# Cross products packed with the diagonal ones, the group norm's sum and its matmul one slab earlier, masks from ScalarE

## The reference, cut to what matters

```python
seg = a_cum[:, :, :, None] - a_cum[:, :, None, :]
decay = exp(where(tril, seg, -inf))          # within a chunk
scores = einsum("bcign,bcjgn->bcijg", C, B)
y_diag = einsum("bcijgr,bcjgrp->bcigrp", scores[..., None] * decay, x * dt)
# from one chunk to the next: states carried with exp of the sums, both directions
v = (y * silu(z)).reshape(b, l, 8, 256)      # group norm
v = v * rsqrt(mean(v * v, axis=-1) + EPS) * g
```

## Time and profile before

| | us |
|---|---|
| median of 3 runs | 2915.68 |
| lowest, highest | 2913.25, 2916.30 |
| the profiled execution | 2910.87 |
| its span, first to last instruction | 2909.1 |
| PE busy | 2869.3 (99%) |
| DVE busy | 1867.6 (64%) |
| ACT busy | 1310.2 (45%) |

### The profile page before, as it was taken

How to read it: one execution, slowest core, us unless ns; L and a number is a source line. 1 busy time by engine, 2 the same in 40 slices (tenths; PEclk the granted TensorE clock), 3 DMA queues, 4 the chain that set the end, 5 groups by cost and what they waited for, 6 DMA issues and landing times.

```text
span 2909.1 us, 34457 instructions
## 1 busy us (share of the span) xinstructions
PE 2869.3 (99%) x12914; PEld 2315.9 (80%) x12914; DVE 1867.6 (64%) x2387; ACT 1310.2 (45%) x1805; POOL 139.5 (5%) x237
## 2 busy tenths in 40 slices
PE   7999999999999999999999999999999999999998
PEld 5888877777778888888888888777777788888887
DVE  5444479999997654444554436889999866554445
ACT  5322256666664434222342224566676534442223
POOL 1000001110001000000000000100100010000000
PEclk9999999999999999999999999999999999999999
DMA  6333233333335433333333333333333463333332
GB/s 194 97 97 95 81 93 100 106 101 96 104 91 180 110 102 94 96 98 96 94 104 99 94 100 95 91 92 90 103 103 96 116 180 92 95 108 95 101 90 84
DMA packets 532024, 301.88 MB, mean 104 GB/s; under 512 B 17039, under 2 KB 521751, under 8 KB 531895
## 3 DMA queue, kind: packets, MB, share of 16 engines
q1 hardware_dynamic: 511888, 261.65, 31.8%
q0 software_dynamic: 17296, 37.29, 4.3%
q10 hardware_dynamic: 2711, 1.21, 0.2%
HBM read 280.54 MB, written 19.53 MB: 103 GB/s over the span
## 4 chain that ended last, share of the span: by engine, by line
PE 83%; ACT 0%; issue 0%; DMA 0%; POOL 0%; DVE 0%; ACTq 0%
PE bank L1270 78%; PE bank L1425 2%; PE bank L1461 1%; PE bank L1401 0%; PE bank L1416 0%; PE bank L1477 0%; PE bank L1469 0%; PE bank L1408 0%; PE bank L1502 0%; DMA LB<-l_image 0%; ACT hhi L800 0%; PE bank L1305 0%; PE bank L1321 0%; POOL RB L401 0%; ACT o_tm L866 0%
## 5 line engine op out<-in xcount | busy, mean ns | idle before, releaser
L1270 PE MATMUL bank<-uhi,whi 128*128 128x512 f32 x1952 | 767.9, 393 | 13.4 <-DVE ulo L938 11.2
L877 DVE TENSOR_TENSOR wlo<-wraw,whi 128x1024 fp32r<-128x1024 f32 x496 | 605.9, 1223 | 266.8 <-ACT whi L505 256.8
L1270 PE MATMUL bank<-hhi,whi 128*128 128x512 f32 x1952 | 767.9, 393 | 2.2 <-ACT tg L710 2.2
L1270 PE MATMUL bank<-ulo,whi 128*128 128x512 f32 x1952 | 761.0, 390 | 0.0
L1270 PE MATMUL bank<-hlo,whi 128*128 128x512 f32 x1952 | 760.7, 390 | 0.0
L1270 PE MATMUL bank<-hhi,wlo 128*128 128x512 f32 x1952 | 760.5, 390 | 0.0
L1270 PE MATMUL bank<-uhi,wlo 128*128 128x512 f32 x1952 | 760.5, 390 | 0.0
L505 ACT ACTIVATE whi<-wraw 128x1024 fp32r<-128x1024 f32 x496 | 521.5, 1054 | 422.6 <-PE bank L1270 405.7
L1270 PEld LDWEIGHTS bank<-uhi,whi 128*128 128x128 f32 x1952 | 367.0, 188 | 101.3 <-issue 11.7
L1270 PEld LDWEIGHTS bank<-hhi,whi 128*128 128x128 f32 x1952 | 366.8, 188 | 89.8 <-issue 11.7
L1270 PEld LDWEIGHTS bank<-uhi,wlo 128*128 128x128 f32 x1952 | 367.0, 188 | 77.4
(11 more groups left out here) (212 smaller groups left out, 1902.3 us busy)
## 6 DMA issues: line engine op xcount, KB each, us to landing
wraw<-in_ffn_w_up SPq DMA_DIRECT2D x179, 512.0 KB, 3.8
wraw<-in_w_in SPq DMA_DIRECT2D x160, 512.0 KB, 4.0
wraw<-in_ffn_w_down SPq DMA_DIRECT2D x64, 512.0 KB, 3.8
wraw<-in_ssd_w_out SPq DMA_DIRECT2D x32, 512.0 KB, 4.4
wraw<-in_ffn_w_down SPq DMA_DIRECT2D x32, 384.0 KB, 3.3
y_spill<-yz POOLq DMA_DIRECT2D x16, 512.0 KB, 3.3
yraw<-y_spill POOLq DMA_DIRECT2D x32, 256.0 KB, 3.9
wraw<-in_conf_w_out SPq DMA_DIRECT2D x16, 512.0 KB, 4.5
```

What stands on the lines that cost most here:

```text
L877: v_.tensor_tensor(wlo[:, t % RING, :], wraw[:, t % RING, :], f32(whi[:, t % RING, :]), ALU.subtract).then_inc(lo_ready, 1)
L1270: ins = t_.matmul(out, a[:, slot, w], b[:, at + k, :], start=start and k == 0 and a is whi and b is hi, stop=stop and k == nk - 1 and a is ...
```

## The change

1. The cross products of a request come right behind its four diagonal ones, in `seg_diag`, into bank4 and bank5 instead of bank2 and bank6. `seg_cross` is gone. ACT takes all six exponentials of a request in step 1 or 3. `seg_diag(0)` waits for both copies of the scores out of banks 4 and 5, and `y_rows(0)`, which writes bank4, for all exponentials of request 1.
2. ACT writes two masks more, into bank2 and bank3, in step 0 behind its copies of the transposed x, in all but the first SSD tile of a layer. PE adds masks in that first tile alone: 8 mask matmuls in all instead of 36.
3. The group norm's sum on DVE moves from the start of step 1 to step 0, behind the taps and ahead of `split`. Its matmul on PE moves from step 1, behind the slab, to step 0, behind the transposes, and goes to bank0 where there is an SSD; there it waits for ACT's read of the slab in bank0, and the slab of step 2 waits for ACT's Ln. In group 9 the matmul stays in step 1 and in bank4.
4. The transposes are written as one accumulation group for each bank.

```diff
@@ ACT, step 0, group with ssd
                             a_.activation(xT[:, 2 * b:2 * b + 2, :], ..., ACT.Copy).then_inc(xt_ready, 1)
+                        if H % NG:
+                            act.wait_ge(xt_ready, H * 2 + 2)
+                            for d in range(2):
+                                mask(0, d)
...
                     if ssd and t in (1, 3):
-                        for e in range(4):
+                        for e in range(EPR):
                             decay(t // 2, e)
-                    if ssd and t in (2, 4):
-                        for e in range(4, EPR):
-                            decay(t // 2 - 1, e)
@@ DVE
-                    if t == 1 and norm:
-
-                        dve.wait_ge(gsq, n * 2 + 2)
-                        v_.tensor_tensor(sq[:, 0, :], sq[:, 0, :], sq[:, 1, :], ALU.add).then_inc(gsq_sum, 1)
...
+                    if t == 0 and norm:
+                        dve.wait_ge(gsq, n * 2 + 2)
+                        v_.tensor_tensor(sq[:, 0, :], sq[:, 0, :], sq[:, 1, :], ALU.add).then_inc(gsq_sum, 1)
@@ PE, seg_diag
-                    by_act = 2 if r else 1 if H % NG else 0
+                    by_act = r or H % NG
...
+                        ins = t_.matmul(bank[4 + c][:, :], LB[rows, H % 2, 1, r, :], RB[rows, H % 2, r, :], start=True, stop=True)
+                        if by_act:
+                            ins.then_inc(seg_ps, 1)
+                    if not by_act:
+                        for c in range(2):
+                            for d in range(2):
+                                t_.matmul(heads(2 + 4 * c + d), identr[:, :], never[:, d, :]..., start=False, stop=True)...
@@ PE, group
                         pe.wait_ge(*free[t])
+                        if t == 2 and norm and ssd:
+                            pe.wait_ge(gln, n + 1)
...
-                    if t == 1 and norm:
+                    if t == (0 if ssd else 1) and norm:
                         pe.wait_ge(gsq_sum, n + 1)
                         if ssd:
-                            pe.wait_ge(sc_ready, H * 2 + 1)
-                        t_.matmul(bank[4][:, :], ones[:, :], sq[:, 0, :], start=True, stop=True).then_inc(gst_ps, 1)
+                            pe.wait_ge(*((tg_ready, G + 1) if slabs else (gate_ready, L * 2 * KD + gate + 1)))
+                        t_.matmul(bank[0 if ssd else 4][:, :], ones[:, :], sq[:, 0, :], start=True, stop=True).then_inc(gst_ps, 1)
                     if t == 1 and ssd:
                         pe.wait_ge(xt_ready, H * 2 + 2)
+                        pe.wait_ge(sc_ready, H * 2 + 2)
...
-                    if t == 2 and ssd:
-                        seg_cross(0)
...
                     if t == 4 and ssd:
-                        seg_cross(1)
-                        if norm:
-                            pe.wait_ge(gln, n + 1)
-                        pe.wait_ge(sc_ready, H * 2 + 2)
+                        pe.wait_ge(e_ready, H * EPG + EPG)
                         y_rows(0)
```

More of the change, by code:

```diff
@@ L258, in masks_by @@
             L, tile = divmod(H, NG)
-            return L * (6 * NG - 2) + 6 * tile + 4 * r
+            return L * (8 * NG - 4) + 8 * tile + 4 * r
         def seg_rows(c, d):
@@ L682, in decay @@
                     else:
-                        dst, src = M[:, r, e - 4, :, 5 - e, :], bank[2 + 4 * (e - 4)]
+                        dst, src = M[:, r, e - 4, :, 5 - e, :], bank[e]
                     a_.activation(dst, src[:, :].rearrange("p (h i) -> p h i", h=HPG), ACT.Exp).then_inc(e_ready, 1)
@@ L730, in group @@
                         need(act, y2_ready, n * 2)
-                        a_.activation(rbc[:, :], bank[4][:, :], ACT.Ln, scale=1.0 / GF, bias=eps_t[:, 0:1]).then_inc(gln, 1)
+                        a_.activation(rbc[:, :], bank[0 if ssd else 4][:, :], ACT.Ln, scale=1.0 / GF, bias=eps_t[:, 0:1]).then_inc(gln, 1)
                         act.wait_ge(gln, n + 1)
@@ L1399, in seg_diag @@
                         for d in range(2):
-                            rows, masked = seg_rows(c, d), c >= 2 - by_act
+                            rows = seg_rows(c, d)
                             ins = t_.matmul(bank[2 + 4 * c + d][:, :], LB[rows, H % 2, 0, r, :], RB[rows, H % 2, r, :],
-                                            start=not masked, stop=masked, skip_group_check=masked)
-                            if r:
+                                            start=not by_act, stop=bool(by_act), skip_group_check=bool(by_act))
+                            if by_act:
                                 ins.then_inc(seg_ps, 1)
[L1405 to L1411, removed]
                     for c in range(2):
-                        pe.wait_ge(e_ready, H * EPG + r * EPR + 2 * c + 1)
                         rows = seg_rows(1 - c, c)
-                        t_.matmul(bank[2 + 4 * c][:, :], LB[rows, H % 2, 1, r, :], RB[rows, H % 2, r, :], start=True, stop=True).then_inc(seg_ps, 1)
+                        ins = t_.matmul(bank[4 + c][:, :], LB[rows, H % 2, 1, r, :], RB[rows, H % 2, r, :], start=True, stop=True)
+                        if by_act:
+                            ins.then_inc(seg_ps, 1)
+                    if not by_act:
+                        for c in range(2):
+                            for d in range(2):
+                                t_.matmul(heads(2 + 4 * c + d), identr[:, :], never[:, d, :].unsqueeze(1).broadcast_to([P, HPG, P]),
+                                          start=False, stop=True).then_inc(seg_ps, 3 if c and d else 1)
                 def y_rows(r):
@@ L1468, in group @@
                             for j in range(2):
-                                ins = t_.transpose(bank[2 + c // 2][:, (c % 2) * GF + j * P:(c % 2) * GF + (j + 1) * P],
-                                                   bc[:, 2 + j, chunk(c)], ident[:, :])
+                                ins = t_.matmul(bank[2 + c // 2][:, (c % 2) * GF + j * P:(c % 2) * GF + (j + 1) * P],
+                                                bc[:, 2 + j, chunk(c)], ident[:, :], start=c % 2 == 0 and j == 0, stop=c % 2 == 1 and j == 1,
+                                                is_transpose=True, skip_group_check=True)
                             if c % 2:
                                 ins.then_inc(xt_ps, 1)
-                    if t == 1 and norm:
+                    if t == (0 if ssd else 1) and norm:
                         pe.wait_ge(gsq_sum, n + 1)
                         if ssd:
-                            pe.wait_ge(sc_ready, H * 2 + 1)
-                        t_.matmul(bank[4][:, :], ones[:, :], sq[:, 0, :], start=True, stop=True).then_inc(gst_ps, 1)
+                            pe.wait_ge(*((tg_ready, G + 1) if slabs else (gate_ready, L * 2 * KD + gate + 1)))
+                        t_.matmul(bank[0 if ssd else 4][:, :], ones[:, :], sq[:, 0, :], start=True, stop=True).then_inc(gst_ps, 1)
                     if t == 1 and ssd:
                         pe.wait_ge(xt_ready, H * 2 + 2)
+                        pe.wait_ge(sc_ready, H * 2 + 2)
                         pe.wait_ge(seg_in[H % 2], (H // 2 + 1) * 8 * 16)
                         seg_diag(0)
-                    if t == 2 and ssd:
-                        seg_cross(0)
                     if t == 3 and ssd:
```

## The result

| | before | changed |
|---|---|---|
| median of 4 runs, us | 2915.24 | 2963.68 |
| lowest to highest | 2913.25 to 2916.30 | 2961.15 to 2964.94 |
| span of the profiled execution | 2909.1 | 2963.0 |
| granted clock, mean | 0.996 | 0.987 |

The changed kernel is slower: ratio 1.0166, 95% interval 1.0148 to 1.0184, 48.4 us at the medians. The two profiled executions are 53.9 us apart in their spans.

The account below looks back on a forecast made before the run. A DVE-PE loop through the norm's sum was to replace PE as the bound: 33.1 us for the loop in both layers, -3.6 PE savings, +10 slower clock, so 2915.7 + 39.5 = 2955 us, range 2937 to 2972.

Parts of the forecast that it names:

- the wait for L1164: Sign: PE's longest waits name DVE's norm sum, about 12 of 3.4 us each and a short one in group 2.
- DVE's 7 us in front of `vp`: Sign: DVE's idle time ahead of `vp` grows from 2.1 to about 6 us.
- the vanished wait of 0.93 us: DVE's wait for the cross products' exponentials goes, since they come a step sooner; 0.93 us less in the loop.
- the case that was forecast: PE stalls for the sum and the clock falls in about half of the stalls: 2955 us; 38%.
- the second rival: Stalls come and the clock falls in each: 2965 us, up to 2975 if DVE's 0.93 wait stays; 22%.
- The loop: DVE from `vp` to the sum, norm's matmul, slab of step 1, back to `vp`: period 57.0 us against 54.14.
- The clock: TensorE slows in half or more of 12 stalls, 1.7 us each, over the slab of step 1: 10 us.
- Ln now runs during the slab of step 1, 5 us ahead of the slab of step 2 that waits for it: ACT's Ln for the norm comes early enough for PE and costs nothing.
- Group 1: The period ending in group 2 grows by 1.0 us in the first layer and 0.3 in the second.
- PE's own work: Were PE alone in charge, 13.9 us less, about 1.5 of it lost to the norm's matmul's change of shape.
- The pair inside the pack: A cross pair run with the diagonal products on PE costs 0.24 us, from nothing to a whole 0.43.
- The rival of 2903: Faster: the sum is in time after all and PE stays in charge, 2915.7 - 12.4 = 2903 us; 6%.

Follow-up runs that it names:

- k5_filled: The changed kernel with eleven unneeded 128x512 matmuls on PE between the transposes and the wait for the sum, 14 times: 2948.9 us.
- k3_norm_alone: The kernel before with only the move of the norm's sum and matmul, cross products and masks as before: 2977.5 us.
- k1_sum_first: The changed kernel with DVE's norm sum ahead of the seven taps of step 0 instead of behind them: 2906.2 us.
- k4_five_taps: The changed kernel with the norm's sum behind five of the seven taps of step 0: 2933.2 us.
- k2_sum_ln_first: The changed kernel with DVE's sum ahead of the taps and ACT's Ln and Exp ahead of the output gate's tanh in group 8: 2899.5 us.
- k8_tg_first: k2_sum_ln_first with ACT's read of the slab of step 0 (tanh into tg, groups 1 to 7) ahead of its split: 2898.4 us.
- k7_norm_alone_good: k3_norm_alone with the sum ahead of the taps and Ln ahead of the output gate's tanh: 2917.3 us.
- k6_masks_pe: k2_sum_ln_first with the masks of banks 2 and 3 added by PE again in 14 tiles: 2903.0 us.

## Why the prediction was right, and where it was off

**Direction and mechanism** came out: the wait for L1164, DVE's 7 us in front of `vp`, the period, and the vanished wait of 0.93 us are the ones named. 2963.7 lies within the range, 9 us above the forecast of 2955. But the case that was forecast, the clock falling in about half of the stalls, is not what happened: it is the second rival, the clock falling in each (2965, given 22%). That the total comes within 2 us of that rival is in part luck: the waits for Ln that were missed (7.5) and a loop that was counted too long (4.7, below) offset each other in part.

**The loop**, term by term: from `vp` to the sum 49.34, measured 49.22 (634.33 to 683.55); sum, release and weight load 0.68 + 0.3, measured 0.74 (683.55 to 684.29); norm's matmul and slab 0.95 + 5.76 = 6.71, measured 6.64 at full clock (511.79 to 518.43). 57.0 against 56.6, which k5_filled then showed whole. The 2.65 us a group taken on average were a little high: at full clock, in k5_filled, the loop is 2.5 us over 54.14 in one of the fullest groups, and 2.26 on average over the six periods of the first layer (norm's matmul at 510.04 in group 2, at 848.44 in group 8). That is 12 x 0.39 = 4.7 us less than counted.

**The clock** is the term that was mis-sized. Counted in half of 12 stalls, 10 us; it fell in all 12, and 12 x 1.6 = 19. The Trainium skill, TensorE: Matmul & The Clock Gate, "HAM oscillation — how this bites in real kernels", describes gaps of a few us that are each followed by a stretch at half rate. By that the forecast would have been the rival of 2965; the changed kernel's trace agrees, with twelve of twelve at 2.65 to 3.4 us of idle time, k3_norm_alone only in nine of twelve. What decides between a fall and none stays open; the length of the stall alone does not, as 3.19 us in k3_norm_alone and 2.9 us in k1_sum_first (L1401, "issue") left the clock at 1.00, while 2.0 us in k4_five_taps brought it down three times.

**Missed**: "Ln now runs during the slab of step 1, 5 us ahead of the slab of step 2 that waits for it". True for groups 2 to 7. In group 8 the output gate's read of the same slab stands ahead of Ln on ACT, and a semaphore wait in an in-order queue is as late as what stands ahead of it. 2 x 2.16 us and twice the clock, 7.5; 6.7 by k1_sum_first less k2_sum_ln_first. ACT's share of 36 in 54 us was no argument.

**Group 1**: the step "1.0 in the first layer, 0.3 in the second" was +3.6 and -1.0: 58.50 (459.93 to 518.43) against 54.92, and 57.22 against 58.17. In the first layer PE stood 2.3 us for the DMA instead of 1.1 and the clock fell behind it; in the second the clock held this time, behind a stall of 2.6 us. Over the twelve profiles this wait for the DMA in the first layer is anything from 0.7 to 2.8 us, so that is the luck of single executions, not the change. The 2.7 us in the second layer, which the prediction puts down to a DMA, are a row of "issue"; the row itself names no DMA.

**PE's own work**, which counts only outside the loop, was put too low: 13.9 - 1.5 = 12.4 us. The balance has 13.9, and the periods, which are cleaner, have more: 54.14 before, 52.97 in k8_tg_first, so 1.17 a group and 16.4 in 14 groups. Its parts:

- Masks: 0.46, measured 0.45.
- The pair inside the pack: 0.24 taken, up to 0.43 allowed, measured 0.22 (0.66 from 692.42 to 693.08, less 0.44).
- The pack as a whole is k7_norm_alone_good against k6_masks_pe. Up to group 4 PE is in charge in both, with periods of 54.19 us (transposes at 510.49, 564.68, 618.87) and 53.42: 0.77 a group, where 0.47 was counted. Of this 0.73 lie between the end of step 1's slab and the one of step 5 (626.06 to 647.51 is 21.45, 624.05 to 644.77 is 20.72). Each change of shape also makes the start of the slab behind it slower (647.51 to 647.85 is 0.34, not 0.23), and two such changes went. The transposes, which only k6_masks_pe has in their new form, take the same in both: 0.88 us to the norm's matmul in group 2 (510.49 to 511.37, 510.23 to 511.11).
- The norm's move costs PE 54.19 - 54.14 = 0.05 us a group, 0.7 in all, not 1.5. From group 4 on the period of k7_norm_alone_good is 54.4 to 54.5; there, too, the norm's matmul comes right behind ACT's read of bank0, 0.99 us behind the transposes instead of 0.88, so this rise is at least in part a wait and not PE's own work:

```profile
618.87 1.04 PE L1476 MATMUL bank<-ident,bc 128*128 128x128 f32 x8
619.14 0.58 ACT L723 ACTIVATE tg<-bank 128x512 f32<-128x512 f32 x1
619.86 1.10 PE L1484 MATMUL bank<-sq,ones 128*128 128x512 f32 x2
```

Together 0.45 + 0.77 - 0.05 = 1.17. The Trainium skill's rule that a weight load overlaps only matmuls in other row groups (same page, "The mechanism") would have put the pair at 0.43; the pack shows 0.22, so here it did not bind.

**The rival of 2903** was not what the changed kernel does, but the price it named was good: k2_sum_ln_first, where PE is in charge, is at 2899.5.

## What to carry to other kernels

Ahead of moving a step forward on the engine that bounds the kernel, ask when its producer's turn comes in the producer's own queue, and what of the bounding engine's work stands behind the wait: if the producer waits in turn for that work, it is a loop, and the engine's shorter queue gives back nothing. Follow the wait through every variant of the stage, the last one too, since another operation may stand ahead of it there. And compare periods in the trace when totals differ by a few us.

## What the runs showed of the hardware

- In the changed kernel TensorE stood 2.65 to 3.4 us in front of a slab twelve times, and each time its clock went to 1.2 GHz for 3.4 us, at a price of 1.6 us. At twelve stalls of 2.5 to 3.2 us in k3_norm_alone it fell nine times, four of them for 6.8 us; at twelve of 1.5 to 2.05 us in k4_five_taps it fell three times.
- Behind the stalls of 2.2 us for ACT's `tg` that every kernel has in both layers, the clock held both times in three of the twelve profiles, fell once in five and twice in four; at 1.6 us each this moves single executions by up to 3.2 us.
- Work that nobody needs, put into such a stall (eleven matmuls, 2.5 us), made the kernel 12 to 15 us faster.
- Six products of 16 rows in four row groups, the last two in groups that the first four use, take 0.66 us from the first start to the next slab's, against 0.44 for four.
